# Mixture-of-experts output: a combining stage replaced by experts that add weighted rows to the output in DRAM

## The chip, the cores and the metric

One core of one Trainium2 chip runs the whole kernel, in float32. The metric is device microseconds of one execution: three timed runs, median 1366.67 us (1364.25 to 1366.97). The granted clock of TensorE averaged 0.947 of full speed.

## The reference

One encoder layer over 1024 tokens of width 1024: a mixer (neighbourhood attention, a bidirectional RWKV-7 scan, memory attention, output projection), then a mixture of experts. Only the second part and its inputs matter here:

```python
x = x + hybrid_mixer(rms_norm(x, attn_norm_w), ...)       # (1, 1024, 1024)
h2 = rms_norm(x, ffn_norm_w)
# 4 groups x 4 experts: best group, its two best experts; weights from the two softmaxes
# every (token, choice) pair is a row for its expert
hid = silu(xb @ w_gate[e]) * (xb @ w_up[e])               # d_ff = 512
y[token] += (hid @ w_down[e]) * weight                    # two contributions for each token
return x + y
```

2048 (token, choice) pairs fall on 16 experts, 128 each on average and unevenly.

## The kernel before, in words

The layer runs in stages: `projection` (with all norms and preparations), `attention`, `scan`, `rwkv_out`, `out_projection_router`, `experts`, `combine`. A stage is a block in which every engine (TensorE `pe`, VectorE `dve`, ScalarE `act`, GpSimd `pool`, SyncE `sp`) has its own instruction list; the order on an engine is the written order, and semaphores are the only link between engines. There is no planner.

**Projection.** GpSimd zeroes a tile (L280) and, once the input rows are normalised, writes it 15 times to the blocks of `expert_rows` that overflow rows may use (L283 to L284, 512 KB each), then fills the attention bias tables with a constant (`bias_background`, 17 transfers). SP loads the weights of each column tile into two buffers (L340), and the products are L483.

**Output projection and router.** TensorE makes the mixer's output rows tile by tile (L1289), VectorE adds `x` into `s.x1`, which stays on the chip, normalises the rows (L1618), and SP stores them to `ffn_rows` in DRAM (L1473). For every pair of tiles VectorE picks the experts (`choose`), their weights (`weigh`, L1579 to L1584) and each choice's slot in its expert's list (`place`, L1590 to L1598). GpSimd scatters token numbers (4 bytes each) to `slot_tokens` at those slots (L1488). At the end SP loads the first 128 slots of each expert as indices (L1477, L1478), and GpSimd gathers the rows of experts 0 and 1 (`expert_rows`, L1676).

**Experts.** Sixteen experts, 128 slots each. On TensorE, a step is: gate product of e (L1812), turning the hidden rows of e-1 (L1790), up product of e (L1820), turning the input of e+1 (L1782), down product of e-1 (L1800). SP loads the weights of e+2 into the buffers that e leaves (three loads of 2 MB, L1669). GpSimd gathers the input of e+2 once the input of e is turned (`pool.wait_ge(x_turned, e - 1)`, two buffers). ACT and VectorE each copy one half of the down product out of PSUM (L1884, L1944), and ACT stores the 128 rows to `expert_rows` (L1886).

**Overflow.** Slots above 128 of an expert are done in blocks of 64 rows, in a loop of 30 conditional turns of which as many are taken as the data ask for (`overflow`, L1727): GpSimd loads 64 slot numbers (L1766), gathers their rows (L1770), TensorE turns them (L1838) and makes the three products (L1845, L1852, L1866), ACT copies and stores the result (L1909, L1912). Every engine walks all 30 turns.

**Combine.** After a barrier of all engines, for each tile of 128 tokens and both choices GpSimd gathers that token's row of `expert_rows` (L2028), VectorE multiplies it by the weight and adds it to `s.x1` (L2038), and SP stores the tile to the output (L2045).

Of the kernel before, what the change touches and what calls it, by code (L numbers as in the profile page):

```python
# [25 lines left out]
ds = bass.ds  # L26
# [28 lines left out]
NBLK = SURE + NOV * ROW // P  # L55
# [136 lines left out]
def projection(nc, s):  # L192
# [6 lines left out]
    with ExitStack() as c:  # L199
# [15 lines left out]
        zeroed, filled, bias_filled, stored = sem("zeroed"), s.filled, s.bias_filled, s.unit_stored  # L215
# [20 lines left out]
        zero = s.proj[:, 0, :]  # L236
# [42 lines left out]
        def _(pool):  # L279
            pool.memset(zero, 0.0).then_inc(zeroed, 1)  # L280
            pool.wait_ge(zeroed, 1)
            pool.wait_ge(row_normed, NORM_TILES)
            for b in range(SURE, NBLK):  # L283
                pool.dma_start(s.y_dram[b * P:(b + 1) * P, :], zero).then_inc(filled, 16)  # L284
            assert bias_background(pool, s, bias_filled) == BIAS_FILLS
            pool.wait_ge(filled, 16 * (NBLK - SURE))
# [241 lines left out]
        def _(act):  # L528
# [54 lines left out]
            for t, col in enumerate(ORDER):  # L583
# [47 lines left out]
                else:  # L631
                    if t == RW_TILES:
                        act.wait_ge(filled, 16 * (NBLK - SURE))
# [775 lines left out]
def out_projection_router(nc, s):  # L1409
# [4 lines left out]
    with ExitStack() as c:  # L1414
# [21 lines left out]
        zeros = sb("zeros", [P, P], I32)  # L1436
        toki = sb("toki", [P, TT], I32)
# [12 lines left out]
        tok = s.tok_dram.rearrange("(e r) o -> r e o", e=NE)  # L1450
# [3 lines left out]
        def _(sp):  # L1454
# [8 lines left out]
            sp.dma_start(s.tok_dram.rearrange("(p n) o -> p (n o)", p=P), zeros[:, :]).then_inc(cleared, 16)  # L1463
# [3 lines left out]
            for t in range(TT):  # L1467
                if t == TT - 1:
                    sp.wait_ge(done, 2 * TT)
                    for load in expert_loads(s, 1, 1)[0:2]:  # L1470
                        load(sp)
                sp.wait_ge(normed, t + 1)
                sp.dma_start(s.h_dram[t * P:(t + 1) * P, :], h[:, t % 2, :]).then_inc(rows_out[t % 2], 16)  # L1473
            for u in range(2):
                sp.wait_ge(rows_out[u], 16 * TT // 2)
            sp.wait_ge(scattered, 16 * 2 * TT)
            sp.dma_start(s.idx[:, 0:2, :], tok[0:P, 0:2, :], allow_slow_non_contiguous=True).then_inc(s.idx_first, 16)  # L1477
            sp.dma_start(s.idx[:, 2:NE, :], tok[0:P, 2:NE, :], allow_slow_non_contiguous=True).then_inc(s.idx_rest, 16)  # L1478

        @block.gpsimd  # L1480
        def _(pool):
            pool.wait_ge(cleared, 16)
            pool.wait_ge(tok_ready, 1)
            for g in range(PAIRS):
                pool.wait_ge(placed, g + 1)
                for t in (2 * g, 2 * g + 1):
                    for k in range(2):
                        pool.indirect_dma_start(out=s.tok_dram, out_offset=bass.IndirectOffsetOnAxis(ap=slot[:, k, t:t + 1], axis=0),  # L1488
                                                in_=toki[:, t:t + 1], in_offset=None).then_inc(scattered, 16)
# [41 lines left out]
        def _(dve):  # L1531
# [43 lines left out]
            def weigh(g):  # L1575
# [7 lines left out]
                link(dve.reciprocal(s.wt[:, 0, two], m1[:, :]))  # L1583
                link(dve.tensor_tensor(s.wt[:, 1, two], s.wt[:, 0, two], e2v[:, :], ALU.mult))  # L1584
# [15 lines left out]
            dve.memset(zeros[:, :], 0).then_inc(zeroed, 1)  # L1600
            dve.tensor_copy(toki[:, :], s.token).then_inc(tok_ready, 1)
            link(dve.memset(s.count[:, :], 0.0))
            dve.wait_ge(router_in, 80)
            for t in range(TT + 2):
# [24 lines left out]
                if t in (4, 6, 8):  # L1629
                    place(t // 2 - 2)  # L1630
            place(PAIRS - 1)
            weigh(PAIRS - 1)
# [41 lines left out]
def expert_rows(s, pool, e):  # L1674

    pool.indirect_dma_start(out=s.expert_x[:, e % 2, :], out_offset=None, in_=s.h_dram,  # L1676
                            in_offset=bass.IndirectOffsetOnAxis(ap=s.idx[:, e, :], axis=0)).then_inc(s.x_in[e % 2], 16)


def experts(nc, s):  # L1680
# [4 lines left out]
    with ExitStack() as c:  # L1685
# [3 lines left out]
        def sem(name):  # L1689
            return c.enter_context(nc.semaphore("ex_" + name))  # L1690
        idx_o = sb("idx_o", [ROW, 2], I32)
# [11 lines left out]
        act_spare = sb("act_spare", [P, 1])  # L1703
# [4 lines left out]
        t16 = sb("t16", [P, 2, TT, NE])  # L1708
        big, base, yslot = (sb(n, [P, 2, TT]) for n in ("big", "base", "yslot"))
# [9 lines left out]
        x_turned, x_copied, gated, upped, silu, hidden, h_turned, h_copied, downed, y_half, y_out = (  # L1719
            sem(n) for n in ("x_turned", "x_copied", "gated", "upped", "silu", "hidden", "h_turned", "h_copied", "downed", "y_half", "y_out"))  # L1720
        step, tables, spared = sem("step"), sem("tables"), sem("spared")
        xo_turned, xo_copied, silu_o, hidden_o, ho_turned, ho_copied, yo_copied, yo_out = (
            sem("o_" + n) for n in ("x_turned", "x_copied", "silu", "hidden", "h_turned", "h_copied", "y_copied", "y_out"))
# [29 lines left out]
        def _(pool):  # L1753
            for u in range(2):
                pool.memset(xo[:, u, :], 0.0).then_inc(zeroed, 1)
            pool.wait_ge(s.idx_rest, 16)
            for e in range(2, NE):
                pool.wait_ge(x_turned, e - 1)
                expert_rows(s, pool, e)
            pool.wait_ge(zeroed, 2)  # L1760
            pool.sem_inc(xo_turned, 2)

            def gather(b, i, u):
                pool.wait_ge(xo_turned, b + 1)
                row = pool.value_load(s.blk[0:1, ds(b + NOV, 1)], min_val=0, max_val=NE * SLOTS - ROW)
                pool.dma_start(idx_o[:, u:u + 1], s.tok_dram[ds(row, ROW), :]).then_inc(idx_in[u], 16)  # L1766
                pool.wait_ge(idx_in[u], i * 16 + 16)
                pool.wait_ge(spared, b + 1)
                pool.tensor_tensor(spare[:, 0:1], s.eps, s.eps, ALU.add).then_inc(spared, 1)
                pool.indirect_dma_start(out=xo[0:ROW, u, :], out_offset=None, in_=s.h_dram,  # L1770
                                        in_offset=bass.IndirectOffsetOnAxis(ap=idx_o[:, u:u + 1], axis=0)).then_inc(xo_in[u], 16)
            pool.sem_inc(spared, 1)
            overflow(pool, gather)

        @block.tensor
        def _(pe):
# [16 lines left out]
            def down(e):  # L1793
                pe.wait_ge(h_copied, e + 1)
                pe.wait_ge(wd_in[e % 2], e // 2 * 16 + 16)
                if e:
                    pe.wait_ge(y_half, e * 2)
# [34 lines left out]
            pe.wait_ge(y_half, 2 * NE)  # L1832

            def block_of_rows(b, i, u):
# [27 lines left out]
                pe.wait_ge(yo_copied, b + 1)  # L1862
# [9 lines left out]
        def _(act):  # L1872
            y_rows = s.y_dram[0:SURE * P, :].rearrange("(b p) n -> b p n", p=P)
            over_rows = s.y_dram[SURE * P:, :].rearrange("(b r) (q n) -> b r q n", r=ROW, q=COLS)

            def finish(e):
# [4 lines left out]
                act.wait_ge(downed, e + 1)  # L1881
                if e:
                    act.wait_ge(y_out, e * 16)
                act.activation(y[:, 0:512], py[:, 0, :], ACT.Copy).then_inc(y_half, 1)  # L1884
                act.wait_ge(y_half, e * 2 + 2)
                act.dma_start(y_rows[e], y[:, :]).then_inc(y_out, 16)  # L1886
# [11 lines left out]
            act.sem_inc(yo_copied, 1)  # L1898

            def block_of_rows(b, i, u):  # L1900
# [6 lines left out]
                act.wait_ge(downed, b + (NE + 1))  # L1907
                act.wait_ge(yo_out, b * 32 + 1)
                act.activation(yo[:, :], py[:, 0, :], ACT.Copy).then_inc(yo_copied, 1)  # L1909
                act.wait_ge(yo_copied, b + 2)  # L1910
                for q in range(COLS):
                    act.dma_start(over_rows[ds(b, 1), :, q, :].rearrange("o r n -> (o r) n"), yo[q * ROW:(q + 1) * ROW, :]).then_inc(yo_out, 16)  # L1912
            act.sem_inc(yo_out, 1)
            n = overflow(act, block_of_rows)
            act.wait_ge(y_out, NE * 16)

            act.wait_ge(yo_out, n * 32 + 1)
            act.activation(act_spare[:, :], s.eps, ACT.Copy)

        @block.vector  # L1920
        def _(dve):
# [18 lines left out]
            def finish(e):  # L1940
                dve.wait_ge(downed, e + 1)
                if e:
                    dve.wait_ge(y_out, e * 16)
                dve.tensor_copy(y[:, 512:1024], py[:, 1, :]).then_inc(y_half, 1)  # L1944
# [23 lines left out]
            def row_of_choice():  # L1968

                link(dve.tensor_tensor(t16[:, :, :, :], s.oh[:, :, :, :], b3(ovn[:, :].unsqueeze(1).unsqueeze(1), [P, 2, TT, NE]), ALU.mult))  # L1970
                link(dve.tensor_reduce(base[:, :, :], t16[:, :, :, :], AX.X, ALU.add))
                link(dve.tensor_scalar(big[:, :, :], s.rank[:, :, :], float(P), None, ALU.is_ge))
                link(dve.scalar_tensor_tensor(out=yslot[:, :, :], in0=s.chosen[:, :, :], scalar=float(P), in1=s.rank[:, :, :], op0=ALU.mult, op1=ALU.add))
                link(dve.tensor_scalar(base[:, :, :], base[:, :, :], float(ROW), float(SURE * P - P), ALU.mult, ALU.add))
                link(dve.scalar_tensor_tensor(out=base[:, :, :], in0=s.chosen[:, :, :], scalar=-float(P), in1=base[:, :, :], op0=ALU.mult, op1=ALU.add))
                link(dve.tensor_tensor(big[:, :, :], big[:, :, :], base[:, :, :], ALU.mult))
                link(dve.tensor_tensor(yslot[:, :, :], yslot[:, :, :], big[:, :, :], ALU.add))
                link(dve.tensor_copy(s.slot[:, :, :], yslot[:, :, :]))

            copy_x(0)  # L1980
            for e in range(NE):
# [13 lines left out]
                if e == 4:  # L1995
                    row_of_choice()
            finish(NE - 1)
            dve.sem_inc(xo_copied, 1)
            dve.sem_inc(hidden_o, 1)

            def block_of_rows(b, i, u):
                dve.wait_ge(xo_turned, b + 3)
# [5 lines left out]
                dve.tensor_tensor(hido[:, :], pu[:, 0:256], sgo[:, :], ALU.mult).then_inc(hidden_o, 1)  # L2008
            overflow(dve, block_of_rows)


def combine(nc, s, out):

    with ExitStack() as c:  # L2014
# [191 lines left out]
```

## Time and profile before

| What | us |
|---|---|
| median of the timed runs | 1366.67 |
| the profiled execution | 1368.25 |
| its span, first to last instruction | 1366.5 |
| TensorE busy | 1204.9 (88%) |
| VectorE busy | 561.3 (41%) |
| ScalarE busy | 311.6 (23%) |
| GpSimd busy | 148.4 (11%) |
| DMA moved | 247 MB, mean 181 GB/s |

Times in the rows are microseconds from the span's start. Busy time is that of compute instructions; waiting and DMA issue are not in it. A landing time runs from the start of a transfer's issue to its semaphore. TensorE's granted clock is given in parts of full speed: 1.00 is 2.4 GHz, 0.50 is 1.2 GHz.

### The profile page before, as it was taken

What the parts mean: (1) busy time and instruction counts of PE and PEld (TensorE: products, weight loads), DVE (VectorE), ACT (ScalarE), POOL (GpSimd) and SP (SyncE); (2) the same over time, 40 slices, a digit from 0 to 9 for tenths busy, and PEclk for the clock granted to TensorE, in tenths of its full rate; (3) what the DMA queues carried; (4) which work ended last, traced back from release to release, by engine and by line L of the source; (5) the groups of instructions that cost most, each with busy time, mean ns of one, the idle gap of its engine ahead of it and who ended that gap; (6) DMA issues with size and microseconds to landing.
All of it is one profiled execution on the core that took longest, in us unless ns stands there. A gap on an engine that the chain in (4) does not pass through costs nothing. (4 is left out here: it accounts for less than half of the span.)

```text
span 1366.5 us, 23919 instructions
## 1 busy us (share of the span) xinstructions
PE 1204.9 (88%) x9780; PEld 678.4 (50%) x9780; DVE 561.3 (41%) x1268; ACT 311.6 (23%) x770; POOL 148.4 (11%) x161
## 2 busy tenths in 40 slices
PE   6989999999998888999887997199999999997840
PEld 5434444444444666999633555044444444444520
DVE  4348355989773544565372345011211011000005
ACT  5243116211205665333301221000000000000000
POOL 0401310300002241000000012200000000100004
PEclk9989999999998999999998997599999999999985
DMA  7641521412115331233309204147888989889939
GB/s 281 250 123 44 167 65 48 137 48 93 47 62 145 95 109 57 81 83 87 129 0 355 96 31 154 46 154 302 344 334 319 360 309 368 306 339 362 404 139 355
DMA packets 107582, 247.01 MB, mean 181 GB/s; under 512 B 33976, under 2 KB 68360, under 8 KB 102104
## 3 DMA queue, kind: packets, MB, share of 16 engines
q1 hardware_dynamic: 90760, 189.63, 38.4%
q0 software_dynamic: 13616, 46.21, 9.9%
q10 hardware_dynamic: 3104, 9.70, 1.8%
q8 instruction: 76, 1.25, 0.4%
q14 instruction: 26, 0.21, 0.1%
HBM read 206.91 MB, written 43.45 MB: 183 GB/s over the span
## 5 line engine op out<-in xcount | busy, mean ns | idle before, releaser
L483 PE MATMUL pj_ps<-hT,pj_w 128*128 128x512 f32 x608 | 270.0, 600 | 5.5 <-DMA pj_w<-in_w_in 5.5
L483 PEld LDWEIGHTS pj_ps<-hT,pj_w 128*128 128x128 f32 x608 | 115.1, 192 | 149.5 <-issue 142.6
L1289 PE MATMUL ps_out<-w_out,mixT 128*128 128x512 f32 x256 | 114.0, 604 | 0.3 <-PEq L1296 0.3
L1800 PE MATMUL ex_py<-wd,ex_hT 128*128 128x512 f32 x256 | 112.6, 593 | 1.4 <-ACT ex_hT L1880 1.4
L1986 DVE TENSOR_TENSOR ex_hid<-ex_pu,ex_sg 128x512 f32<-128x512 f32 x16 | 11.1, 691 | 212.3 <-PE ex_pu L1820 212.3
L1289 PEld LDWEIGHTS ps_out<-w_out,mixT 128*128 128x128 f32 x256 | 49.4, 195 | 61.1 <-issue 61.1
L692 DVE RECIPROCAL mixT<-mixT 128x1024 f32<-128x1024 f32 (+1 forms) x11 | 68.9, 6262 | 25.8 <-ACT mixT L611 25.7
L1800 PEld LDWEIGHTS ex_py<-wd,ex_hT 128*128 128x128 f32 x256 | 47.5, 190 | 55.7 <-issue 54.0
L1812 PE MATMUL ex_pg<-proj 128*128 128x512 f32 x128 | 57.9, 606 | 1.3 <-DVE proj L1938 1.3
L1884 ACT ACTIVATE proj<-ex_py 128x512 f32<-128x512 f32 x16 | 9.6, 598 | 215.8 <-PE ex_py L1800 215.8
L1812 PE MATMUL ex_pg<-mixT,proj 128*128 128x512 f32 x128 | 56.3, 593 | 1.3 <-DVE proj L1938 1.3
L1820 PE MATMUL ex_pu<-mixT,proj 128*128 128x512 f32 x128 | 56.3, 592 | 0.0
L1820 PE MATMUL ex_pu<-proj 128*128 128x512 f32 x128 | 56.3, 592 | 0.0
L487 PE MATMUL pj_ps<-proj,hT 128*128 128x512 f32 x128 | 55.4, 593 | 0.0
L1239 DVE TENSOR_TENSOR sc_lm<-sc_ps,cst 128x384 f32<-128x384 f32 x64 | 35.7, 557 | 39.7 <-PE sc_ps L1176 38.5
L1488 POOL DMA_INDIRECT slot_tokens<-op_toki,op_slot x16 | 15.6, 974 | 317.1 <-DVE op_slot L1597 313.4
L1944 DVE COPY proj<-ex_py 128x512 f32<-128x512 f32 x16 | 11.1, 692 | 93.4 <-PE ex_py L1800 93.4
L1676 POOL DMA_INDIRECT expert_x<-ffn_rows,idx x16 | 15.1, 941 | 276.1 <-PE ex_pt L1782 263.7
L1782 PE MATMUL ex_pt<-cst,expert_x 128*128 128x128 f32 x128 | 17.5, 282 | 28.4 <-PEq L1724 28.4
L1172 PE MATMUL sc_ps<-proj 64*64 64x128 f32 x512 | 40.8, 270 | 1.0 <-PEq L1149 1.0
L1812 PEld LDWEIGHTS ex_pg<-proj 128*128 128x128 f32 x128 | 24.9, 195 | 32.8 <-issue 31.1
L1812 PEld LDWEIGHTS ex_pg<-mixT,proj 128*128 128x128 f32 x128 | 24.2, 190 | 31.7 <-issue 30.1
(302 smaller groups left out, 1947.4 us busy)
## 6 DMA issues: line engine op xcount, KB each, us to landing
wd<-in_moe_w_down SPq DMA_DIRECT2D x21, 2048.0 KB, 10.1
proj<-in_moe_w_gate SPq DMA_DIRECT2D x11, 2048.0 KB, 14.4
proj<-in_moe_w_up SPq DMA_DIRECT2D x11, 2048.0 KB
mixT<-in_moe_w_gate SPq DMA_DIRECT2D x10, 2048.0 KB, 14.6
mixT<-in_moe_w_up SPq DMA_DIRECT2D x10, 2048.0 KB
pj_w<-in_w_in SPq DMA_DIRECT2D x19, 512.0 KB, 3.8
products<-pj_unit POOLq DMA_DIRECT2D x4, 2048.0 KB, 10.2
proj<-products SPq DMA_DIRECT2D x32, 256.0 KB, 3.0
```

What stands on the lines that cost most here:

```text
L483: mm = pe.matmul(ps[:, t % 2, half, :], w[:, t % 2, n, :], s.hT[:, n, half * 512:(half + 1) * 512], start=(n == 0), stop=(n == KD - 1))
L487: mm = pe.matmul(ps[:, t % 2, half, :], s.hT[:, n, b * P:(b + 1) * P], w_v[:, n, :], start=(n == 0), stop=(n == KD - 1))
L692: then(dve.reciprocal(std[:, 0:ln], std[:, 0:ln]))
L1172: pe.matmul(ps[p0:p1, n, 0, m * P:(m + 1) * P].rearrange("p (f t) -> p f t", f=2), f[p0:p1, n, 2 + m, :], f[p0:p1, n, 0:2, :], start=True, ...
L1239: dve.tensor_tensor(lm[:, i % 2, n, :, :].rearrange("p f c -> p (f c)"), ps[:, n, 0, 0:6 * HD], s.l_mask[UNITS[n][0]], ALU.mult).then_inc( ...
L1289: mm = pe.matmul(s.ps_out[:, t % 2, half * 512:(half + 1) * 512], s.mixT[:, k, t * P:(t + 1) * P], s.w_out[:, k, half * 512:(half + 1) * 5 ...
L1488: pool.indirect_dma_start(out=s.tok_dram, out_offset=bass.IndirectOffsetOnAxis(ap=slot[:, k, t:t + 1], axis=0), in_=toki[:, t:t + 1], in_o ...
L1676: pool.indirect_dma_start(out=s.expert_x[:, e % 2, :], out_offset=None, in_=s.h_dram, in_offset=bass.IndirectOffsetOnAxis(ap=s.idx[:, e, : ...
L1782: mm = pe.transpose(pt[:, j // 4, (j % 4) * P:(j % 4 + 1) * P], x[:, e % 2, j * P:(j + 1) * P], s.ident)
L1800: mm = pe.matmul(py[:, half, :], hT[:, j, :], wd[e % 2][:, j, half * 512:(half + 1) * 512], start=(j == 0), stop=(j == KF - 1))
L1812: mm = pe.matmul(pg[:, :], xT[:, u, j, :], wg[u][:, j, :], start=(j == 0), stop=(j == KD - 1))
L1820: mm = pe.matmul(pu[:, :], xT[:, u, j, :], wu[u][:, j, :], start=(j == 0), stop=(j == KD - 1))
```

## The change

The output tensor itself becomes the accumulator.

- The combine stage, `expert_rows`, its zero fill, and the table that names each choice's row in it (`row_of_choice`) are gone.
- The router also stores `s.x1` (mixer result) to the output, behind each store of `ffn_rows` on SP.
- A slot holds 8 words instead of 1: row numbers to read and to write, of the whole row and of its two halves, and the weight. Unused slots carry weight 0 and write numbers beyond the output, which the scatter skips. The last `weigh` comes before the last `place`.
- Each expert reads its 128 rows of the output, VectorE computes product x weight + rows in one operation from PSUM, and GpSimd scatters the sum back. Since two experts may add to one token, the scatter has landed before the next read is issued, in one GpSimd loop that also gathers the inputs:

```diff
-            for e in range(2, NE):
-                pool.wait_ge(x_turned, e - 1)
-                expert_rows(s, pool, e)
+            for e in range(NE):
+                read_rows(e)
+                if e + 2 < NE:
+                    pool.wait_ge(x_turned, e + 1)
+                    expert_rows(s, pool, e + 2)
+                if e == NE - 2:
+                    pool.wait_ge(zeroed, 2)
+                    pool.wait_ge(tables, 1)
+                    gather(0, 0, 0, 1)
+                write_rows(e)
```

with

```diff
+            def read_rows(e):
+                pool.indirect_dma_start(out=acc, in_=rows, in_offset=(s.idx[:, e, ROW_READ])).then_inc(acc_in, 16)
+            def write_rows(e):
+                pool.wait_ge(summed, e + 1)
+                pool.indirect_dma_start(out=rows, out_offset=(s.idx[:, e, ROW_WRITE]), in_=y,
+                                        bounds_check=SEQ - 1, oob_is_err=False).then_inc(s.row_written, 16)
+                pool.wait_ge(s.row_written, 16 * (e + 1))
```

(offset arguments abridged). On VectorE and ACT:

```diff
-                act.activation(y[:, 0:512], py[:, 0, :], ACT.Copy).then_inc(y_half, 1)
-                act.dma_start(y_rows[e], y[:, :]).then_inc(y_out, 16)
-                dve.tensor_copy(y[:, 512:1024], py[:, 1, :]).then_inc(y_half, 1)
+                dve.wait_ge(acc_in, 16 * (e + 1))
+                dve.scalar_tensor_tensor(out=y, in0=py, scalar=weight[:, e:e + 1], in1=acc, op0=ALU.mult, op1=ALU.add).then_inc(summed, 1)
```

The overflow blocks do the same with half rows, two halves of 64 rows side by side on 128 partitions. Block b's turn on GpSimd:

```diff
+            def rest(b, i, u):
+                pool.indirect_dma_start(out=acc_o, in_=halves, in_offset=(idx_o[:, u, HALF_READ])).then_inc(s.half_in[u], 16)
+                pool.wait_ge(xo_turned, b + 1)
+                gather(b + 1, 1 - u, i + u, b * 3 + 2)     # two index lists, wait, input rows of b+1
+                pool.wait_ge(summed_o, b + 2)
+                pause(b * 3 + 3)                            # a one-column add
+                pool.indirect_dma_start(out=halves, out_offset=(idx_o[:, u, HALF_WRITE]), in_=yo, ...).then_inc(s.row_written_o[u], 16)
+                pool.wait_ge(s.row_written_o[u], i * 16 + 16)
+                pause(b * 3 + 4)
```

Before, the gather of block b waited only for block b-1's input to be turned.

## Rows read from the trace of the kernel before

**Rows 1.** Page part 2: span in 40 slices, busy tenths.

```profile
PE   6989999999998888999887997199999999997840
```

**Rows 2.** Windows: stretch, length, busy (instructions) by engine, clock, DMA share, GB/s.

```profile
905.00:1242.00 337.00, 333.62 (x908) 156.54 (x906) 45.57 (x70) 26.48 (x47) 14.66 (x18) 1.00 0.82 319
1327.50:1366.50 39.00, 0.00 (x0) 0.00 (x0) 20.50 (x16) 0.20 (x1) 17.92 (x16) 0.50 0.85 323
```

**Rows 3.** Timeline of one expert step: start, us, engine, line, operation.

```profile
1158.27 1.04 PE L1782 MATMUL ex_pt<-cst,expert_x 128*128 128x128 f32 x8
1159.58 0.94 POOL L1676 DMA_INDIRECT expert_x<-ffn_rows,idx  x1 [20.98 <-PE ex_pt L1782]
...
1166.21 0.38 SPq L1669 DMA_DIRECT2D wd<-in_moe_w_down  x1
1166.94 0.34 ACTq L1886 DMA_DIRECT2D expert_rows<-proj  x1
...
1176.40 0.94 POOL L1770 DMA_INDIRECT ex_xo<-ffn_rows,ex_idx_o  x1 [0.15 <-issue]
...
1180.19 1.04 PE L1782 MATMUL ex_pt<-cst,expert_x 128*128 128x128 f32 x8
...
1187.93 1.45 PE L1812 MATMUL ex_pg<-proj 128*128 128x512 f32 x3
```

**Rows 4.** View of DMA issues, expert steps: last number is us to landing.

```profile
expert_rows<-proj ACTq DMA_DIRECT2D x1, 512.0 KB, 8.1
...
expert_x<-ffn_rows,idx POOLq DMA_INDIRECT x1, 6.7
...
ex_xo<-ffn_rows,ex_idx_o POOLq DMA_INDIRECT x1, 10.4
```

**Rows 5.** The same view where nothing else moved: 1329 us, and 43 us.

```profile
proj<-expert_rows,slot POOLq DMA_INDIRECT x1, 4.1
...
expert_rows<-proj POOLq DMA_DIRECT2D x1, 512.0 KB, 3.1
```

**Rows 6.** Timeline, prices on VectorE, and the scatter of slot tokens.

```profile
59.86 1.28 DVE L683 SCALAR_TENSOR_TENSOR proj<-pj_ps,par,proj 128x1023 f32<-128x1023 f32 x1 [10.05 <-ACT proj L630]
...
856.06 0.16 DVE L1584 TENSOR_TENSOR wt<-wt,op_e 128x2 f32<-128x2 f32 x1
...
859.25 0.96 POOL L1488 DMA_INDIRECT slot_tokens<-op_toki,op_slot  x1 [0.30 <-issue]
...
869.99 0.38 SPq L1477 DMA_DIRECT2D idx<-slot_tokens  x1
```

**Rows 7.** View of windows, a step's loads ending; after a short TensorE stop.

```profile
1162.00:1165.00 3.00, 3.00 (x8) 1.33 (x7) 0.00 (x0) 0.00 (x0) 0.58 (x1) 1.00 0.71 281
...
1242.00:1250.20 8.20, 6.71 (x35) 4.35 (x37) 0.69 (x1) 0.00 (x0) 0.57 (x1) 0.58 1.02 434
```

**Rows 8.** View of windows, projection, around its one long TensorE stop.

```profile
71.50:77.04 5.54, 0.01 (x1) 0.00 (x0) 5.43 (x5) 3.46 (x3) 0.00 (x0) 0.60 0.64 238
77.04:80.00 2.96, 2.96 (x4) 1.41 (x5) 0.94 (x1) 1.99 (x3) 0.00 (x0) 0.50 0.26 32
```

**Rows 9.** View of DMA issues, projection weights at 58.6 us.

```profile
pj_w<-in_w_in SPq DMA_DIRECT2D x1, 512.0 KB, 18.4
```

**Rows 10.** Timeline of the overflow blocks.

```profile
1259.57 1.09 PE L1838 MATMUL ex_pt<-cst,ex_xo 128*128 128x128 f32 x8
...
1273.94 1.10 PE L1838 MATMUL ex_pt<-cst,ex_xo 128*128 128x128 f32 x8
...
1282.64 0.93 POOL L1770 DMA_INDIRECT ex_xo<-ffn_rows,ex_idx_o  x1 [0.15 <-issue]
...
1317.24 0.60 ACT L1909 ACTIVATE ex_yo<-ex_py 128x512 f32<-128x512 f32 x1 [3.83 <-PE ex_py L1866]
```

**Rows 11.** View of DMA issues, an overflow index list at 1262 us.

```profile
ex_idx_o<-slot_tokens POOLq DMA_DIRECT2D x1, 0.2 KB, 5.7
```

**Rows 12.** View of one line: GpSimd leaving the expert block.

```profile
L1685 POOLq DRAIN  x1: 2018/2018/2018, 1292.5 to 1292.5; - x1
```

More of the change, by code:

```diff
@@ L1582, in weigh @@
                 link(dve.tensor_tensor(m1[:, :], m1[:, :], den[:, :], ALU.mult))
-                link(dve.reciprocal(s.wt[:, 0, two], m1[:, :]))
-                link(dve.tensor_tensor(s.wt[:, 1, two], s.wt[:, 0, two], e2v[:, :], ALU.mult))
+                link(dve.reciprocal(wt[:, 0, two], m1[:, :]))
+                link(dve.tensor_tensor(wt[:, 1, two], wt[:, 0, two], e2v[:, :], ALU.mult))
+                for col in (WEIGHT, WEIGHT + NEXT_HALF):
+                    link(dve.tensor_copy(entry[:, two, :, col].bitcast(F32), wt[:, :, two].rearrange("p k t -> p t k")))
             def place(g):
@@ L1598, in place @@
                 link(dve.tensor_tensor(s.count[:, :], pl[:, 1, 3 * NE:4 * NE], s.count[:, :], ALU.add))
-            dve.memset(zeros[:, :], 0).then_inc(zeroed, 1)
-            dve.tensor_copy(toki[:, :], s.token).then_inc(tok_ready, 1)
+            link(dve.memset(unused[:, :, :], 0))
+            link(dve.memset(unused[:, :, HALF_WRITE], 2 * SEQ))
+            link(dve.memset(unused[:, :, HALF_READ + NEXT_HALF], 1))
+            link(dve.memset(unused[:, :, HALF_WRITE + NEXT_HALF], 2 * SEQ + 1))
+            dve.memset(unused[:, :, ROW_WRITE], SEQ).then_inc(zeroed, 1)
+            token = s.token.unsqueeze(2).to_broadcast([P, TT, 2])
+            for col in (HALF_READ, HALF_WRITE):
+                link(dve.tensor_scalar(entry[:, :, :, col], token, 2.0, None, ALU.mult))
+                link(dve.tensor_scalar(entry[:, :, :, col + NEXT_HALF], token, 2.0, 1.0, ALU.mult, ALU.add))
+            link(dve.tensor_copy(entry[:, :, :, ROW_READ], token))
+            dve.tensor_copy(entry[:, :, :, ROW_WRITE], token).then_inc(tok_ready, 1)
             link(dve.memset(s.count[:, :], 0.0))
@@ L1690, in sem @@
             return c.enter_context(nc.semaphore("ex_" + name))
-        idx_o = sb("idx_o", [ROW, 2], I32)
+        idx_o = sb("idx_o", [P, 2, ENTRY], I32)
+        acc, acc_o = s.proj[:, 0, :], s.proj[:, 1, 0:512]
+        weight = s.idx[:, :, WEIGHT].bitcast(F32)
+        weight_o = idx_o[:, :, WEIGHT].bitcast(F32)
         x, x_in = s.expert_x, s.x_in
@@ L1753, in _, with pause, gather @@
         def _(pool):
+            def read_rows(e):
+                pool.indirect_dma_start(out=acc, out_offset=None, in_=rows,
+                                        in_offset=bass.IndirectOffsetOnAxis(ap=s.idx[:, e, ROW_READ:ROW_READ + 1], axis=0)).then_inc(acc_in, 16)
+            def write_rows(e):
+                pool.wait_ge(summed, e + 1)
+                pool.indirect_dma_start(out=rows, out_offset=bass.IndirectOffsetOnAxis(ap=s.idx[:, e, ROW_WRITE:ROW_WRITE + 1], axis=0),
+                                        in_=y, in_offset=None, bounds_check=SEQ - 1, oob_is_err=False).then_inc(s.row_written, 16)
+                pool.wait_ge(s.row_written, 16 * (e + 1))
+            def pause(count):
+                pool.wait_ge(spared, count)
+                pool.tensor_tensor(spare[:, 0:1], s.eps, s.eps, ALU.add).then_inc(spared, 1)
+            def gather(b, u, behind, count):
+                row = pool.value_load(s.blk[0:1, ds(b + NOV, 1)], min_val=0, max_val=NE * SLOTS - ROW)
+                pool.dma_start(idx_o[0:ROW, u, :], s.tok_dram[ds(row, ROW), :]).then_inc(idx_in[u], 16)
+                pool.dma_start(idx_o[ROW:P, u, 0:NEXT_HALF], s.tok_dram[ds(row, ROW), NEXT_HALF:2 * NEXT_HALF]).then_inc(idx_in[u], 16)
+                pool.wait_ge(idx_in[u], behind * 32 + 32)
+                pause(count)
+                pool.indirect_dma_start(out=xo[0:ROW, u, :], out_offset=None, in_=s.h_dram,
+                                        in_offset=bass.IndirectOffsetOnAxis(ap=idx_o[0:ROW, u, ROW_READ:ROW_READ + 1], axis=0)).then_inc(xo_in[u], 16)
+            pool.sem_inc(spared, 1)
             for u in range(2):
@@ L1906, in block_of_rows @@
                 act.activation(hoT[:, :], ph[:, 0:256], ACT.Copy).then_inc(ho_copied, 1)
[L1907 to L1918, printed above, removed]
+            overflow(act, block_of_rows)
         @block.vector
@@ L1941, in finish @@
                 dve.wait_ge(downed, e + 1)
-                if e:
-                    dve.wait_ge(y_out, e * 16)
-                dve.tensor_copy(y[:, 512:1024], py[:, 1, :]).then_inc(y_half, 1)
+                dve.wait_ge(acc_in, 16 * (e + 1))
+                dve.scalar_tensor_tensor(out=y, in0=py[:, :, :].rearrange("p a n -> p (a n)"), scalar=weight[:, e:e + 1], in1=acc, op0=ALU.mult, op1=ALU.add).then_inc(summed, 1)
             def overflow_blocks():
@@ L2060, in hybrid_layer @@
     s.h_dram = dram("ffn_rows", (SEQ, D))
[L2061 to L2062 removed]
+    s.tok_dram = dram("slot_tokens", (NE * SLOTS, ENTRY), I32)
+    s.out = out
     s.p_dram = dram("products", (4, NCH, P, 4 * CHUNK))
@@ L2132, in hybrid_layer @@
         experts(nc, s)
-        combine(nc, s, out)
 def constants(np):
```

140 lines of the change are left out of this document (42 added, 98 removed).

## The prediction

> **What bounds the kernel now.** I read the page's slices first, then the expert stage by windows and timeline, then the landing times of its transfers, last the waits that close each block.
>
> The slices show TensorE busy nearly throughout; in the last one it does nothing [rows 1]. From 905 to 1242 us it is busy 333.6 of 337 us at full clock, with the DMA engines at 0.82; the combining stage is 39.0 us in which it does nothing [rows 2]. So the 16 expert steps are TensorE's, and combining is a tail of its own.
>
> A step is 21.9 us (down product's end at 1166.2, the next at 1188.1). I count from that end, as +t. At +0 SP issues three weight loads (6 MB), and one DMA stage issues the expert's rows at +0.7; TensorE turns the next expert's input at +14.0 and then does the down product of the one before; GpSimd's gather for the turn after next is issued 1.3 us after a turn, so at +15.3, with 20.6 us in hand [rows 3]. It lands 6.7 us later, at +22.0 [rows 4]. The cover of that gather is what the change touches.
>
> **Zero fill.** Fifteen 512 KB writes from GpSimd at 43 us go. The projection load issued at 58.6 us takes 18.4 us to land [rows 9], and TensorE, waiting for it, stands still for 5.5 us; the products behind it then run at 1.2 GHz, from 77.04 to about 82.8 us in the windows, so 5.8 us of work at half rate cost 2.9 [rows 8]. The 2.6 MB of bias fill stay, but alone they are gone by then: I take both away, 5.5 + 2.9 = **-8.4 us**. TensorE has no other long wait in the projection, so the shift should survive. Bounds: 0 (the bias fill alone still delays the load) to -10.
>
> **Router.** Copying output rows to DRAM (8 x 512 KB on SP) and clearing 512 KB instead of 64 KB go beside products. The last weights are now made before the last slots: five small operations and two copies at about 0.2 us each [rows 6], on the path to the last scatters: **+1.4 us**. Slot entries grow from 4 to 32 bytes; the count of descriptors is the same, so I leave the index loads' price. Bounds: 0 to +4. The table work at expert 4 goes from VectorE, which is idle there anyway: 0.
>
> **The 16 experts.** ACT's and VectorE's copies out of PSUM become one 128x1024 multiply-add: 1.28 us for such an operation with a PSUM operand [rows 6], against about 0.7 us each. TensorE waits for it only before the next down product, 15 us later: 0. The sum also waits for the output rows; behind it on VectorE stand the next input's copy and the next hidden product. By the times below the rows land before +21, so this wait hides.
>
> GpSimd's queue is where it hurts. Its loop for expert e reads output rows, gathers the input of e+2, waits for the sum of e, scatters it, and waits until that has landed. So the gather for e+2 stands behind the landed scatter of e-1, whose sum comes only at the end of TensorE's step e. From that end:
> - sum: 1.3 us; GpSimd starts the scatter at +1.6.
> - scatter landed: the trace has no 4 KB-row scatter. The nearest in bytes, direction and moment is the store at +0.7, 8.1 us [rows 4]. Quiet neighbours are a 512 KB store from GpSimd at 3.1 and a gather of such rows at 4.1 [rows 5]; the other end is the last scatter of slot tokens, issued at 859.25 with its waiter free only at 869.9: 10.7 us with the DMA engines idle [rows 6]. I take 8.4, the middle of that store over the steps: landed at +10.0.
> - next iteration: read issued at +10.3 (0.94 us, then 0.3 of issue), input gather issued at +11.5.
> - input landed: two gathers bracket it. The one issued at +10.2 took 10.4 us [rows 3, 4], so landed at +20.6; the one at +15.3 landed at +22.0. The weights end about +19 [rows 7], and the new 512 KB read pushes that by about 1.2 us. I take **+21.0**.
>
> The turn wants it at +14.0, so TensorE waits 7.0 us. Behind two such stops the clock fell: 0.58 over 8.2 us in one case, 0.50 in the other [rows 7, 8]. I charge 4.4 us of the turn and down product at 1.2 GHz: +2.2. The step is then 21.9 + 7.0 + 2.2 = 31.1 us. This holds for iterations 1 to 13 (inputs of experts 3 to 15): 13 x 9.2 = **+120 us**. The ends: quiet prices for both (scatter 4.1, two gathers 5.3) give an input at +12.5 and no wait; 10.7 and 10.4 give +24.2, and 13.2 us a step.
>
> The Trainium skill ("DMA: Bandwidth & Descriptors", section "Specifications") says that a transfer in pieces under 512 B is read, modified and written. That would explain the 10.7 us of the token scatter, and speaks for not pricing a 4 KB-row scatter by it; it would then be rows 4 or 5.
>
> **Last expert to first block.** Iteration 14 also fetches an index list, waits for it and gathers block 0's rows before it may scatter; the scatter of 14 so starts at about +22.6 of step 15, lands at +31, and the read of 15 lands at about +38.5, its sum at +39.8. Today TensorE is free at +30.9. **+9 us** (0 to +12).
>
> **Overflow blocks.** There are five (21 loads of each weight for 16 experts). A block is 14.4 us of TensorE [rows 10]. Now block b+1's index list is fetched only after block b-1's scatter landed. From the sum of b-1: pause 0.7, scatter 8.4, pause and branches 0.9, read 1.2, reading the row number 1.3, two list loads 1.2, landing 5.7 [rows 11], pause 0.4, gather 8.5 (between 6.7 and 10.4), together 28; then block b+1 itself and its sum, 15.2. So every sum comes at least 43 us after the last but one, where two blocks are 28.8 now. Chained from the last expert's sum, with the last two rounds at half-quiet prices: sums at 20, 43, 63, 81 and 96 us, where the fifth comes at 76 now. **+20 us** (+1 at quiet prices, +35 at the loaded ones throughout).
>
> **Tail.** Now: last matmul 1317.1, end 1366.5. Then: sum 0.8, wait and pause 0.7, scatter 4.1 quiet [rows 5], 0.3, the 25 branches not taken, which cost GpSimd 8.9 us between its last gather and its drain [rows 10, 12], and 0.5 to close: 1332.4. **-34 us** (-27 if the scatter takes 10.7).
>
> **Sum.** -8.4 + 1.4 + 120 + 9 + 20 - 34 = +108. The profiled execution took 1368.25 us (span 1366.5 and 1.75 around it), 1.6 above the median of the three runs, so 1368.25 + 108 - 1.6 = 1474.7: **1475 us**.
>
> **Rivals.**
> - *The round trip fits* (chance 0.12). If the software queue is served in turn with the weight loads, the prices are the quiet ones, inputs land by +12.5 and no step waits. Then -8.4 + 1.4 + 0 + 0 + 5 - 34 = -36: 1331 us. It decides at an input by +14.0. For it: 4.1 and 3.1 us [rows 5]. Against it: every transfer of 256 KB or more issued within the first 15 us of a steady step took 8.1 us or more [rows 4]. The Trainium skill (same page, "Anatomy of one DMA — SWDGE (gpsimd) path") fits such a transfer as 2.0 us plus bytes over 436 GB/s, by which 512 KB is 3.2 us, and would side with this rival; in the trace only the quiet ones agree.
> - *Half of it* (0.20). The scatter at 8.4 us, but the gather lands at its usual 6.7: input at +18.2, wait 4.2, and the clock holds. 13 x 4.2 = 55; with +5 and +8 behind: -8.4 + 1.4 + 55 + 5 + 8 - 34 = +27: 1394 us. For it: 6.7 us is the price of this very gather today [rows 4]. Against it: the gather at +10.2 carried half the bytes and took 10.4.
> - *As forecast* (0.55), 1435 to 1510 us.
> - *Slow scatter* (0.10): 10.7 us like the token scatter, inputs at +24.2: 13 x 13.2 = 172, +12, +30, tail -27.5: +179: 1546 us.
> - *The change doesn't do what it says*, for instance the gain of the zero fill lost because the bias fill alone blocks the load: +8 on any case (0.03 left over for it and for others).
>
> **Range and chances.** 1385 to 1530 us takes in the forecast and most of the half case, and leaves out the fitting round trip and the slow scatter. About 0.2 % (2.7 us) is what runs of this kernel can tell from none. Faster 0.13 (the first rival), the same 0.02, slower 0.85.
>
> **What would show each step.** In the profile after: TensorE waiting at the turn of the input (L1782's line) for expert_x, 13 times, about 7 us each, with the clock under 1 behind it; GpSimd waiting for the landing of its own scatter, about 7 us after its issue; steps of 31 us between down products; no stop at 71 us in the projection; less than 16 us behind the last matmul. The forecast is wrong if steps stay 21.9 us, which needs scatter plus gather to land within 12.4 us of the sum, or if the clock stays up (then 29 us a step and 1446 us).

## The result, and the profile after

| | before | after |
|---|---|---|
| median of the runs, us | 1366.32 (1364.25 to 1366.97) | 1491.74 (1489.96 to 1496.95) |
| profiled execution, span, us | 1366.5 | 1490.6 |
| ratio after / before | | 1.0928, 95% interval 1.0907 to 1.0948 |
| forecast | | 1475, range 1385 to 1530 |

The medians take in the profiled execution beside the three timed runs. The change costs 125 us. The page of the changed kernel, parts 1, 2 and 4:

```profile
PE 1241.5 (83%) x9780; PEld 698.1 (47%) x9780; DVE 554.9 (37%) x1265; ACT 297.8 (20%) x748; POOL 170.3 (11%) x190
...
PE   6999999999979899998799477777776777774673
...
PEclk9999999999989999999899679899898888987986
...
DMA 20%; PE 16%; issue 2%; DVE 2%; POOL 1%; POOLq 0%; ACT 0%; DVEq 0%; ACTq 0%
DMA out<-proj,idx 11%; PE ex_py L1843 8%; DMA expert_x<-ffn_rows,idx 6%; PE ex_pt L1825 2%; PE ex_pg L1855 2%; PE ex_pu L1863 1%; DVE proj L1965 1%; PE ex_pg L1888 1%; DMA out<-ex_yo,ex_idx_o 1%; POOL proj L1766 1%; PE ex_py L1909 1%; DMA ex_idx_o<-slot_tokens 1%; DMA proj<-out,idx 1%; DMA ex_xo<-ffn_rows,ex_idx_o 1%; PE ex_pu L1895 1%
```

Where the expert slices stood at 9 [rows 1] they now stand mostly at 7, and the closing stretch without TensorE is down from 49.4 to 19.1 us. In the chain that ended last the largest share is the landing of the scatter (`out<-proj,idx`, 11%), and of the other waits the largest is the landing of the input gather (`expert_x<-ffn_rows,idx`, 6%). The waits (engine, line, waited for: us in total, times, longest) name the same two:

```profile
POOL proj L1766 <- DMA out<-proj,idx: 160.7, 15, 11.6
...
PE ex_pt L1825 <- DMA expert_x<-ffn_rows,idx: 103.5, 13, 8.5
```

One step in the timeline, to set beside [rows 3]:

```profile
1101.68 7.03 PE L1855 MATMUL ex_pg<-proj 128*128 128x512 f32 x16
1101.87 0.38 SPq L1678 DMA_DIRECT2D wd<-in_moe_w_down  x1
1101.88 1.28 DVE L1965 SCALAR_TENSOR_TENSOR proj<-ex_py,idx,proj 128x1024 f32<-128x1024 f32 x1 [6.40 <-PE ex_py L1843]
...
1103.99 1.01 POOL L1771 DMA_INDIRECT out<-proj,idx  x1 [19.81 <-DVE proj L1965]
...
1116.22 0.97 POOL L1766 DMA_INDIRECT proj<-out,idx  x1 [11.22 <-DMA out<-proj,idx]
1117.49 0.94 POOL L1685 DMA_INDIRECT expert_x<-ffn_rows,idx  x1 [0.30 <-issue]
1124.05 1.97 PE L1825 MATMUL ex_pt<-cst,expert_x 128*128 128x128 f32 x8 [8.04 <-DMA expert_x<-ffn_rows,idx]
1125.82 8.98 PE L1843 MATMUL ex_py<-wd,ex_hT 128*128 128x512 f32 x16
1134.64 0.59 PE L1855 MATMUL ex_pg<-mixT,proj 128*128 128x512 f32 x1
```

The scatter goes out 2.3 us after the down product's end, the queue moves on 12 us later, only then does the input gather go, and TensorE has stood for 8.0 us when it lands. The turn then takes 1.97 instead of 1.04 us and the down product about 9 instead of 7: the clock has fallen. From 905 us to the last step, in windows (columns as in [rows 2], where the clock was 1.00):

```profile
905.00:1329.00 424.00, 320.48 (x790) 152.55 (x789) 46.63 (x55) 14.11 (x26) 37.82 (x39) 0.87 0.62 241
```

The spans part into stretches that add up to the whole difference (from marks in the timelines; the forecast's terms beside them):

| stretch | before | after | difference | forecast |
|---|---|---|---|---|
| start to first expert's turn | 881.9 | 864.3 | -17.6 | -7.0 |
| first turn to gate product of expert 15 | 327.9 | 464.8 | +136.9 | +120 |
| to the first block's turn | 32.6 | 46.3 | +13.7 | +9 |
| five blocks, to the last matmul | 74.7 | 96.1 | +21.4 | +20 |
| last matmul to end | 49.4 | 19.1 | -30.3 | -34 |
| sum | | | +124.1 | +108 |

The total is nearer than its terms: the start was 10.6 us better than forecast, the four stretches behind it together 26.7 us worse.

### The profile page after: what moved, and what is told of

Its sections match the earlier page's. It is cut to its first block and busy times, and to the rows that moved or that the text cites. A ratio compares the mean times of both kernels' runs of the same rounds, so it can differ in the third digit from the quotient of the medians.

```text
span 1490.6 us, 23875 instructions
## 1 busy us (share of the span) xinstructions
PE 1241.5 (83%) x9780; PEld 698.1 (47%) x9780; DVE 554.9 (37%) x1265; ACT 297.8 (20%) x748; POOL 170.3 (11%) x190
## 5 line engine op out<-in xcount | busy, mean ns | idle before, releaser
L1843 PE MATMUL ex_py<-wd,ex_hT 128*128 128x512 f32 x256 | 130.8, 669 | 1.0 <-DVE proj L1965 1.0
L1825 PE MATMUL ex_pt<-cst,expert_x 128*128 128x128 f32 x128 | 29.6, 407 | 121.9 <-DMA expert_x<-ffn_rows,idx 103.5
L1926 ACT ACTIVATE ex_sg<-ex_pg 128x512 f32<-128x512 f32 x16 | 9.6, 597 | 454.9 <-PE ex_pg L1855 454.9
L1843 PEld LDWEIGHTS ex_py<-wd,ex_hT 128*128 128x128 f32 x256 | 55.5, 224 | 66.8 <-issue 65.6
L1825 PEld LDWEIGHTS ex_pt<-cst,expert_x 128*128 128x128 f32 x128 | 23.8, 212 | 133.8 <-DMA expert_x<-ffn_rows,idx 114.3
L1960 DVE COPY proj<-ex_pt 128x1024 f32<-128x1024 f32 x16 | 19.6, 1225 | 137.6 <-PE ex_pt L1825 137.4
L1965 DVE SCALAR_TENSOR_TENSOR proj<-ex_py,idx,proj 128x1024 f32<-128x1024 f32 x16 | 20.5, 1284 | 123.6 <-PE ex_py L1843 102.8
L1486 POOL DMA_INDIRECT slot_tokens<-op_entry,op_slot x16 | 15.6, 973 | 316.2 <-DVE op_slot L1597 312.6
L1771 POOL DMA_INDIRECT out<-proj,idx x16 | 16.1, 1008 | 292.9 <-DVE proj L1965 292.9
## 6 DMA issues: line engine op xcount, KB each, us to landing
proj<-in_moe_w_up SPq DMA_DIRECT2D x11, 2048.0 KB, 18.3
```

The source lines that it names most:

```text
L1825: mm = pe.transpose(pt[:, j // 4, (j % 4) * P:(j % 4 + 1) * P], x[:, e % 2, j * P:(j + 1) * P], s.ident)
L1843: mm = pe.matmul(py[:, half, :], hT[:, j, :], wd[e % 2][:, j, half * 512:(half + 1) * 512], start=(j == 0), stop=(j == KF - 1))
L1960: dve.tensor_copy(xT[:, e % 2, :, :].rearrange("p a b -> p (a b)"), pt[:, :, :].rearrange("p a b -> p (a b)")).then_inc(x_copied, 1)
L1965: dve.scalar_tensor_tensor(out=y, in0=py[:, :, :].rearrange("p a n -> p (a n)"), scalar=weight[:, e:e + 1], in1=acc, op0=ALU.mult, op1=ALU ...
```

## The experiments

The theory after the result: the steps lengthen because the input gather of expert e+2 stands in GpSimd's queue behind the landed scatter of e-1, and the fallen clock adds to it. Rival 1: the added traffic (a 512 KB read and a row scatter a step) slows the loads in any order. Rival 2: VectorE's bigger sum, or the late reading of the output rows, holds up the down product. Ratios are to the kernel before, measured on the same chip each time. A line of dots in a cut of code stands for lines left out.

### Input gathers one expert further ahead

```diff
                 read_rows(e)
-                if e + 2 < NE:
-                    pool.wait_ge(x_turned, e + 1)
-                    expert_rows(s, pool, e + 2)
+                if e == 0:
+                    pool.wait_ge(x_turned, 1)
+                    expert_rows(s, pool, 2)
+                if e + 3 < NE:
+                    pool.wait_ge(x_turned, e + 2)
+                    expert_rows(s, pool, e + 3)
```

> From the changed kernel: GpSimd's queue runs its input gathers one expert further ahead (iteration e gathers the input of e+3, before the scatter of e), so that no input gather stands behind a landed scatter; rows read, rows scattered, sums and bytes are the same. Theory (order in the queue): the gather is issued right after a turn again, as in the kernel before, the 13 waits of 7.6 to 8.5 us at the turn go, the clock stays up, and a step takes 21.9 instead of 32.3 us: 1491.7 - 13 x 10.4 = 1356 us, a little less if the last expert's junction gains too (1345 to 1362), under the kernel before. Rival 1 (added traffic: 1 MB more a step slows weights and gathers whatever the order): steps stay over 27 us, 1420 us or more. Rival 2 (the bigger sum on VectorE or the late rows read hold up the down product): steps over 27 us too, with the wait at the down product or at the sum and not at the turn.

Measured: 1362.5 us, ratio 0.9924 (0.9900 to 0.9949), against 1.0928. Its windows up to the last step:

```profile
905.00:1217.00 312.00, 312.00 (x848) 146.57 (x847) 49.12 (x58) 15.20 (x28) 40.14 (x43) 1.00 0.89 349
```

TensorE is busy in all of the 312 us at full clock, a step takes 21.9 us, and the wait at the turn is gone. The whole is 0.8% faster than the kernel before, although the DMA engines now carry everything that the change added: 0.89 busy and 349 GB/s, against 0.82 and 319 before [rows 2]. The landings (issue view, last number us) show how long each transfer still takes:

```profile
out<-proj,idx POOLq DMA_INDIRECT x4, 10.8
proj<-out,idx POOLq DMA_INDIRECT x3, 6.3
expert_x<-ffn_rows,idx POOLq DMA_INDIRECT x3, 6.3
```

A scatter of 10.8 us holds up nobody when nothing urgent stands behind it. Both rivals fall: each had put the steps over 27 us whatever the order.

### The wait alone, in the kernel before

```diff
                 pool.wait_ge(x_turned, e - 1)
+                if e >= 3:
+                    pool.wait_ge(y_out, 16 * (e - 2))
                 expert_rows(s, pool, e)
```

> From the kernel before: GpSimd's gather of expert e's input (e of 3 and up) waits for the landed store of expert e-3's rows as well, so it stands behind a landed write as in the changed kernel; no byte more is moved. Theory (the wait itself): the store is issued at about +0.7 of a step and lands about 8 us later, the gather goes at about +9.2 and takes 8 to 10 us there, the input comes at +18 to +19.5 where it is wanted at +14: a stop of 4 to 5.5 us a step and up to 2 of low clock behind it, 13 x 4.5 to 7 = 60 to 90 us, 1425 to 1457 us. Rival 1 (the added traffic is what lengthens the steps): 1366 us, steps of 21.9 us.

Measured: 1486.4 us, ratio 1.0837 (1.0819 to 1.0855): +115 us from one wait and no byte. Its step:

```profile
1113.43 0.34 ACTq L1888 DMA_DIRECT2D expert_rows<-proj  x1
...
1122.65 0.94 POOL L1676 DMA_INDIRECT expert_x<-ffn_rows,idx  x1 [29.70 <-DMA expert_rows<-proj]
1133.64 1.57 PEld L1784 LDWEIGHTS ex_pt<-cst,expert_x 128*128 128x128 f32 x8 [7.63 <-DMA expert_x<-ffn_rows,idx]
1133.64 1.97 PE L1784 MATMUL ex_pt<-cst,expert_x 128*128 128x128 f32 x8 [6.80 <-DMA expert_x<-ffn_rows,idx]
```

Steps are 30.7 us (weight loads issued at 928.54 and 1327.86, 13 steps), +8.8 each, 6.6 of it waiting at the turn. The expectation (60 to 90 us, at most 1457 us) was too small: the store took 8.5 us in the median, the gather so went at about +10 and took 10.8, where +9.2 and 8 to 10 had been put down. The same gather takes 6.6 us in the kernel before, where it is issued at +15.3 [rows 3, 4]. So a delay costs twice here, by itself and by a slower landing earlier in the step. 115 of the 137 us of the expert stretch are shown without any scatter. The rest fits the input's landing still later in the changed kernel, at +22.3 instead of about +21: its scatter goes out at +2.3 where the store goes at +0.7, and takes 12 us. No run separates these two.

### The zero fill put back

```diff
...
+            for b in range(15):
+                pool.dma_start(s.y_dram[b * P:(b + 1) * P, :], zero).then_inc(filled, 16)
             assert bias_background(pool, s, bias_filled) == BIAS_FILLS
+            pool.wait_ge(filled, 16 * 15)
```

> From the changed kernel: the fifteen 512 KB writes of zeros at 43 us are put back, into a DRAM tensor that nobody reads, with the wait on them that the kernel before had. As predicted: the projection load issued at 58.6 us lands late again, TensorE stops 5.5 us and runs 5.8 us of work at half clock: +8.4, 1500.1 us. Rival: the shift comes from elsewhere or is made up later in the projection: within 1.5 us of 1491.7.

Measured: 1499.4 us, ratio 1.0937 (1.0918 to 1.0955). The stop is back, 7.1 us long where the kernel before had 5.5:

```profile
PE pj_ps L485 <- DMA pj_w<-in_w_in: 7.1, 1, 7.1
```

The run to set beside it is that of the first experiment, on the same chip and without the fill. Against it a product of the projection starts 6.4 us later (94.53 against 88.08) and the index loads 5.6 us later (861.91 against 856.36). The mechanism holds; how much it is worth depends on the clock. Without the fill TensorE still pauses 1.3 us for ScalarE just before 70 us, and behind that the clock was low in one execution and full in another. The first line is that of the first experiment, the second that of the unaltered changed kernel run again:

```profile
71.00:77.00 6.00, 6.00 (x8) 2.41 (x8) 5.89 (x5) 3.45 (x3) 0.00 (x0) 0.50 0.19 18
71.00:77.00 6.00, 6.00 (x15) 2.58 (x14) 5.89 (x6) 3.44 (x3) 0.00 (x0) 1.00 0.15 14
```

The first profile of the changed kernel lies between them, at 0.72. The same product starts at 93.74 us in the kernel before, at 86.66 in that profile, and at 85.38 in the one at full clock (on another chip): 7.1 and 8.4 us earlier. So the 2.9 us charged to the clock are gained in some executions and not in others, and why the clock fell in some and not in others is open. The whole times don't tell any of it: 1.0937 against 1.0928 and 1.0917 lies inside their intervals.

### The unaltered changed kernel, again

> The changed kernel, unaltered, beside the others of this job, so that its ratio to the kernel before and its marks are taken on the same chip as theirs. Expected: the ratio of 1.093 again. If the zero fill is worth 5.5 to 6.5 us as the marks of the first four runs say, its ratio lies 0.004 to 0.005 below that of the kernel with the fill put back (1.0937): 1.089; if it is worth 8.4, 1.0875; if nothing, 1.0937.

Measured: 1490.9 us, ratio 1.0917 (1.0875 to 1.0959), executions from 1480.4 to 1495.5. It spreads more than the kernel before: where the blocks fall against their own scatters varies (block 2's turn comes 40 us after block 0's here, 45 in the first profile). The ratio's interval takes in all three expected values, so it decides nothing on the zero fill. A few us can't be read from whole times of this kernel, only from its rows.

### Slot entries: wide, apart, two words

The first two are from the kernel before. Both widen the clearing write and change the index loads to suit. First, 32-byte entries:

```diff
-                                                in_=toki[:, t:t + 1], in_offset=None)
+                                                in_=toki[:, t, :], in_offset=None)
...
-    s.tok_dram = dram("slot_tokens", (NE * SLOTS, 1), I32)
+    s.tok_dram = dram("slot_tokens", (NE * SLOTS, ENTRY), I32)   # ENTRY = 8
```

> From the kernel before: slot entries are 8 words of 4 bytes instead of one (the clearing write, the token scatters and the index loads with them), nothing else. If the width of an entry is what lets the last token scatter land 2.2 instead of 10.7 us after its issue in the changed kernel: 1366.3 - 8.5 = 1357.8 us. Rival (the shorter landing comes with something else of the change, such as the output rows' copies or the zero fill): 1366.3 us, or up to 1 us more for the larger clear.

Measured: 1357.5 us, ratio 0.9895 (0.9878 to 0.9912), faster than the kernel before by 14 us, where 8.5 were expected. Its last scatter and the index load (SP issues that load once all sixteen scatters have landed; the profile gives no landing of a single one):

```profile
860.82 0.96 POOL L1490 DMA_INDIRECT slot_tokens<-op_toki,op_slot  x1 [0.30 <-issue]
...
862.98 0.38 SPq L1479 DMA_DIRECT2D idx<-slot_tokens  x1
```

2.2 us where the kernel before had 10.7 [rows 6]; on the chip of this run the kernel with the wait alone, whose entries are packed 4-byte ones, had 14.5 (858.97 to 873.46). That is 12.3 us of the 14. Another 2 follow the layout too: from this load to the first turn of an input it is 9.8 us here, and 11.9 in both kernels with packed 4-byte entries. Then 4 bytes written, 32 bytes apart:

```diff
-                dve.tensor_copy(slot[:, :, two], slotf[:, :, :])
+                dve.tensor_scalar(slot[:, :, two], slotf[:, :, :], float(APART), None, ALU.mult)   # APART = 8
...
-    s.tok_dram = dram("slot_tokens", (NE * SLOTS, 1), I32)
+    s.tok_dram = dram("slot_tokens", (NE * SLOTS * APART, 1), I32)
```

> From the kernel before: slot entries stay 4 bytes wide, but stand 32 bytes apart (slot number times 8, a clear of 512 KB, strided index loads). It tells the width of a written entry from its neighbours. If the 10.7 us landing of the last token scatter comes from the narrow write itself: it stays at 10 us or more and the time within 2 us of the kernel before (ratio 0.999 to 1.002). If it comes from entries sharing a 32-byte line with those that other descriptors write: 2.2 us as in the kernel with 32-byte entries, ratio 0.99.

Measured: 1357.1 us, ratio 0.9923 (0.9899 to 0.9948), again 2.2 us (858.72 to 860.96), and again 9.8 us to the first turn. Between 4 and 32 bytes the width of a write doesn't matter; how near its neighbours stand does. At last, packed entries of 8 bytes, in the kernel with 32-byte ones:

```diff
-ENTRY = 8
+ENTRY = 2
```

> From the kernel before: slot entries of 8 bytes (two words), packed. With packed 4-byte entries the last token scatter landed 10.7 to 14.5 us after its issue, with entries 32 bytes apart 2.2 us, whether 4 or 32 bytes were written. If it is the number of entries that share 32 bytes (8 before, 4 now): between the two, 4 to 8 us. If any sharing costs the whole: over 9 us. If only 4-byte neighbours do: 2.2 us.

Measured in a single execution of 1377.8 us: the index load came 20.6 us after the last scatter, longer than with 4 bytes.

```profile
853.69 0.97 POOL L1490 DMA_INDIRECT slot_tokens<-op_toki,op_slot  x1 [0.30 <-issue]
...
874.25 0.38 SPq L1479 DMA_DIRECT2D idx<-slot_tokens  x1
```

So packed 8-byte entries are as slow as 4-byte ones or slower, as the second expectation had it ("any sharing costs the whole: over 9 us"). That they are slower rests on one execution, and there the DMA engines were still busy with earlier work at first:

```profile
854.00:860.00 6.00, 0.00 (x0) 0.00 (x0) 0.00 (x0) 0.00 (x0) 0.66 (x1) 0.50 0.91 121
860.00:874.00 14.00, 0.00 (x0) 0.00 (x0) 0.00 (x0) 0.00 (x0) 0.00 (x0) 0.50 0.03 2
```

In the 14 us after that they were all but idle, and the scatters had still not landed. Distances between 8 and 32 bytes were not run, so these runs do not say where slow ends, nor what makes it slow.

### Fewer empty turns

```diff
-            with eng.Fori(0, NOV // 2) as i:
+            with eng.Fori(0, NOV // 10) as g:
+                with eng.If(g * 10 < n):      # then ten guarded turns as before
```

> From the changed kernel: the 30 guarded turns of the overflow loop are put in three groups of ten with a guard around each, so that after the fifth block 5 turns and two groups are passed over instead of 25 turns. If the 8.3 us between the last landed scatter and GpSimd's drain are those turns (0.33 us each): 18 turns fewer, 6 us less, 1485.7 us (ratio to the changed kernel 0.996). Rival: they are a fixed cost of closing, or the drain grows by as much: 1491.7 us.

Measured: 1492.2 us, ratio 1.0925 (1.0888 to 1.0961), so no gain that whole times show. The rows show one: from GpSimd's last pause to the end the changed kernel takes 1475.94 to 1490.6, this one 1481.11 to 1490.3, 14.7 against 9.2 us. The 5.5 us are gained in the tail and lost in the spread of the blocks ahead of it. What stays is GpSimd's closing drain of 6.1 us in both:

```profile
L1694 POOLq DRAIN  x1: 6102/6102/6102, 1484.3 to 1484.3; - x1
```

### Lists and inputs of the blocks ahead too

From the first experiment: four list buffers; blocks 0 to 2's lists at expert 8, inputs of blocks 0 and 1 at expert 10, and in block b (arguments abridged):

```diff
-                pool.wait_ge(xo_turned, b + 1)
-                gather(b + 1, 1 - u, i + u, b * 3 + 2)
+                pool.wait_ge(xo_turned, b + 2)
+                pool.wait_ge(idx_in[(q + 2) % 4], ...)
+                pause(b * 3 + 2)
+                input_rows(u, (q + 2) % 4)      # input of b+2
+                lists(b + 3, (q + 3) % 4)
```

> From the kernel with its input gathers one expert further ahead (1362.5 us, 0.9924 of the kernel before): the overflow blocks get the same treatment. The index lists of blocks 0 to 2 and the inputs of blocks 0 and 1 are fetched during experts 8 and 10, and block b then gathers the input of b+2 and fetches the lists of b+3 (four list buffers), so neither stands behind a landed scatter. Theory (order in GpSimd's queue, in the blocks too): first turn to last matmul goes from 101 us to about 14.4 + 4 x 15.5 = 77 us (a block's chain is then scatter 6, read 6, sum and pauses 3.5, just over TensorE's 14.4), so 24 us less: about 1338 us (0.976); the 17 us in which TensorE waits for the sum of expert 15 stay. Rival (the blocks are held by the round trip of scatter and read itself, which stays): 95 us or more for the blocks, 1357 us or more.

Measured: 1344.7 us, ratio 0.9830 (0.9797 to 0.9863). From the first block's turn to the last sum it is 87.4 us, down from 101.2: between the 77 of the theory and the 95 of the rival. TensorE no longer waits for a block's input; two of five sums wait for the half rows instead:

```profile
1279.00 0.75 DVE L2033 SCALAR_TENSOR_TENSOR ex_yo<-ex_py,ex_idx_o,proj 128x512 f32<-128x512 f32 x1 [9.51 <-DMA proj<-out,ex_idx_o]
...
1297.33 0.75 DVE L2033 SCALAR_TENSOR_TENSOR ex_yo<-ex_py,ex_idx_o,proj 128x512 f32<-128x512 f32 x1 [7.25 <-DMA proj<-out,ex_idx_o]
```

Sum to sum there is 19.0 and 18.3 us, of which the read takes 9.8 and 9.0 where 6 had been put down. For these two blocks the round trip through DRAM is the limit, once the order in the queue is mended; the other two sums came 17.0 and 14.4 us after the one before, held by TensorE.

### Both, with grouped turns

From the experiment before:

```diff
-            with eng.Fori(0, (NOV + 3) // 4) as i:
+            with eng.Fori(0, (NOV + 7) // 8) as g:
+                with eng.If(g * 8 < n):       # then eight guarded turns
```

> The kernel with input gathers and list loads ahead (0.983 of the kernel before) with the guarded turns grouped as well, in four groups of eight: after the fifth block 3 turns and 3 groups are passed over instead of 27 turns. The grouping took 5.5 us off the span between the last landed scatter and the end (14.4 to 9.0 us) in the changed kernel. Theory: 5 to 6 us less than with the lists ahead alone, ratio 0.979 (0.976 to 0.982), 1338 us. Rival (the turns passed over stand beside something else that ends no earlier): 0.983.

Measured: 1341.1 us, ratio 0.9792 (0.9776 to 0.9808): 2.1% under the kernel before and, by the two ratios, 10% under the changed one. The tail is 9.8 us (1325.40 to 1335.2), from 15.4.

## Why the prediction was right, and where its terms were off

**The mechanism** is as forecast: the landed scatter in front of the input gather, 13 stops at L1825 of 7.6 to 8.5 us (7.0 forecast), a fall of the clock with each, steps of 32.3 us (31.1 forecast). It is shown from both sides: reordering alone takes the steps back to 21.9 us, and the wait alone, in the kernel before, makes them 30.7.

**The step's size**: 9.2 us forecast, 10.4 measured, 16 us over 13 steps; this is the largest part of what the forecast fell short by. The scatter was priced at 8.4 us by the store of [rows 4]; its landings are 12.0 us in the median. It starts at +2.3 rather than +1.6. Against that, the gather landed in 6.5 us, not 9.5. It now starts at +15.8, close to the +15.3 at which the kernel before pays 6.6. These are errors of opposite sign, and that the wait came out only 1 us off is partly luck. The rival called the slow scatter was nearer on the scatter (10.7 us), and put 10.4 us on the gather, which was wrong. The clock cost 2.4 us a step (10.4 less 8.0 of waiting), 2.2 forecast.

The Trainium skill ("DMA: Bandwidth & Descriptors", section "Anatomy of one DMA — SWDGE (gpsimd) path") gives, as an estimate by its fit, 3.2 us for 512 KB and 2.6 for 256 KB. The last scatter, of 256 KB with nothing beside it, landed in 2.4 us, in agreement; the 512 KB scatters under the weight stream took 12, and that of expert 15, which met only the end of a weight load, came near with 3.8. The first rival failed because it took quiet prices for loaded steps.

**Zero fill**: -8.4 forecast, -6 to -8.4 shown. The stop went; the low clock stayed in some executions and not in others.

**Router**: the last weights cost 0.6 us where 1.4 was forecast (marks 7.7 us early at 804 us are 7.1 early at the last slots), but the entries' layout, left at nothing, was worth 8.5 to 12.3 us in the landing of the scatters and 2 more behind it. This is the one step that failed outright: "the count of descriptors is the same, so I leave the index loads' price". The prediction looked at the loads and not at the landing that they wait for, whose odd 10.7 us stood in [rows 6]. It used the rule of the Trainium skill ("DMA: Bandwidth & Descriptors", section "Specifications") on pieces under 512 B to explain that figure. But 32-byte entries and 4-byte ones standing apart are under 512 B too and land in 2.2 us, so the rule alone does not explain it. What differs between the runs is how near the entries stand.

**Junction**: +9 forecast, +13.7 measured. The scatter of 14 started at +23.4 (+22.6 forecast) and landed at +32.4 (+31); the rows of 15 then took 10.9 us where 7.5 were put down. **Blocks**: +20 and +21.4; TensorE waited 15.8 us for block inputs in three waits. **Tail**: -34 and -30.3. The prediction's own sign, less than 16 us behind the last matmul, did not come: it was 19.1. GpSimd's drain took 6.1 us ([rows 12] had 2.0) where 0.5 had been put down for closing; the last scatter, a little faster than priced, gave some of it back.

**What hid** in the steps, as forecast: the 1.28 us sum and the reading of the rows before it. TensorE's down product waited for a sum once, 1.0 us at expert 15; the first block then stood behind the last sum, as the junction's term says.

## What to carry to other kernels

Before moving a landed wait into an engine's queue, list what is issued behind it, and issue first whatever another engine will want; the same transfers in another order were worth 9% here (0.9924 against 1.0928). Price a transfer by its kind and its place in the step: the gather took 6.6 or 10.8 us by when it was issued, the scatter of the same 512 KB 3.8 or 12. A chain of read, sum and write through DRAM has a length of its own (18 to 19 us a block here, beside weight loads) which no order in the queue removed, so give it work that is longer than that.

## What the runs showed of the hardware

- After the last scatter of slot entries, all had landed 10.7 to 14.5 us after its issue where 4-byte entries were packed, 20.6 us where 8-byte ones were (one execution), and 2.2 us where entries stood 32 bytes apart, whether 4 or 32 bytes wide. For the last 9 us or more of the slow ones the DMA engines were near idle (share 0.00 from 860 to 869 us in the kernel before).
- GpSimd's drain at the end of the expert block took 6.1 us in five profiles of kernels of the changed form (6.5 in the two where more was fetched ahead) although its last wait was over; in the five profiles of the form before it took 2.0. No run says what in the change makes the difference.
- A guarded turn passed over cost GpSimd about 0.3 us: 20 turns fewer, and three group guards more, took 5.5 us off.
- The DMA engines carried 349 GB/s for 312 us beside a TensorE that never stopped: the steps had room for the added traffic.
